# Expert gates: one-hot matmuls replaced by indirect DMAs that add chosen gates into zeroed DRAM tables

## The reference

```python
def peer_ffn(h, wq, subkeys, u, v):        # h: (1, 512, 1024)
    q = (h @ wq).reshape(B, T, 8, 2, 128)
    s = jnp.einsum('bthpd,pnd->bthpn', q, subkeys)      # 8 heads, 2 sides, 128 sub-keys
    s_top, i_top = lax.top_k(s, 16)
    cand = s_top[..., 0, :, None] + s_top[..., 1, None, :]        # 256 candidates
    cand_idx = i_top[..., 0, :, None] * 128 + i_top[..., 1, None, :]
    best, pos = lax.top_k(cand.reshape(B, T, 8, 256), 16)
    experts = jnp.take_along_axis(cand_idx.reshape(B, T, 8, 256), pos, axis=-1)
    gates = jax.nn.softmax(best, axis=-1)
    # y[t] = sum over the 128 picks k of  gates[t,k] * gelu(h[t] . u[e_k]) * v[e_k]
```

## Time and profile before

| | |
|---|---|
| times of three runs | 3919.15, 3919.49, 3920.51 us |
| span of the profiled execution, first to last instruction | 3916.3 us |
| PE busy | 3864.7 us, 99% of the span |
| DVE busy | 2781.5 us, 71% |
| ACT busy | 1523.5 us, 39% |
| POOL busy | 1321.6 us, 34% |
| mean granted TensorE clock | 0.997 |

### The profile page before, as it was taken

One profiled execution on the slowest core, in us unless ns is written; L12 is line 12 of the kernel. 1 busy time (PEld: TensorE's weight loads), 2 busy tenths in 40 slices (PEclk: granted clock), 3 DMA queues, 4 the chain that ended last, 5 costly groups with the idle time before them and its releaser, 6 DMA issues.

```text
span 3916.3 us, 48823 instructions
## 1 busy us (share of the span) xinstructions
PE 3864.7 (99%) x18074; PEld 3129.0 (80%) x18074; DVE 2781.5 (71%) x4585; ACT 1523.5 (39%) x2251; POOL 1321.6 (34%) x758
## 2 busy tenths in 40 slices
PE   7999999999999999999999999999999999999999
PEld 5767878888888888888877678788888888888887
DVE  5736557987777758888776363589787776588886
ACT  4537433343333333333344373433433333433332
POOL 2432333440000017777334223334300000387772
PEclk9999999999999999999999999999999999999999
DMA  7635333667776579999746432237677765899995
GB/s 286 226 124 170 113 128 108 226 228 263 266 260 222 204 260 391 364 359 358 269 162 222 134 130 81 82 118 242 232 260 262 258 241 180 305 376 372 353 354 198
DMA packets 411869, 918.97 MB, mean 235 GB/s; under 512 B 38416, under 2 KB 176528, under 8 KB 410032
## 3 DMA queue, kind: packets, MB, share of 16 engines
q1 hardware_dynamic: 327664, 664.77, 49.2%
q0 software_dynamic: 45056, 134.38, 9.2%
q10 hardware_dynamic: 38976, 117.66, 7.8%
HBM read 794.00 MB, written 256.90 MB: 268 GB/s over the span
## 4 chain that ended last, share of the span: by engine, by line
PE 83%; issue 7%; DVE 4%; POOL 4%; ACT 1%; DMA 1%; ACTq 0%; POOLq 0%; SPq 0%; DVEq 0%
PE ps L1057 14%; PE ps L1058 14%; PE ps L1059 14%; PE ps L1075 10%; PE ps L1077 10%; PE ps L1076 10%; POOL w_lo L1007 4%; PE ps L1432 2%; PE ps L1333 1%; PE ps L1337 1%; PE ps L1335 1%; PE ps L1300 1%; PE ps L1314 1%; PE ps L1290 1%; PE ps L1251 1%
## 5 line engine op out<-in xcount | busy, mean ns | idle before, releaser
L598 ACT ACTIVATE w_hi<-raw 128x1024 fp32r<-128x1024 f32 x504 | 534.3, 1060 | 1595.1 <-PE ps L1059 1316.1
L1057 PE MATMUL ps<-h_hi,w_hi 128*128 128x512 f32 x2768 | 1086.5, 393 | 5.1 <-POOL w_lo L1007 3.5
L1058 PE MATMUL ps<-h_hi,w_lo 128*128 128x512 f32 x2768 | 1080.1, 390 | 0.0
L1059 PE MATMUL ps<-h_lo,w_hi 128*128 128x512 f32 x2768 | 1079.5, 390 | 0.0
L1007 POOL TENSOR_TENSOR w_lo<-raw,w_hi 128x1024 fp32r<-128x1024 f32 x242 | 614.4, 2539 | 1101.1 <-ACT w_hi L598 1101.1
L1012 POOL DMA_INDIRECT acts<-expert_act,e_act x256 | 381.6, 1491 | 1244.9 <-DMA expert_act<-gel 1167.5
L1057 PEld LDWEIGHTS ps<-h_hi,w_hi 128*128 128x128 f32 x2768 | 519.2, 188 | 122.4 <-issue 8.9
L1059 PEld LDWEIGHTS ps<-h_lo,w_hi 128*128 128x128 f32 x2768 | 518.5, 187 | 112.2
L1058 PEld LDWEIGHTS ps<-h_hi,w_lo 128*128 128x128 f32 x2768 | 518.8, 187 | 100.9
L1867 DVE TENSOR_TENSOR w_lo<-raw,w_hi 128x1024 fp32r<-128x1024 f32 x192 | 235.1, 1224 | 277.1 <-ACT w_hi L598 277.1
L1020 POOL DMA_INDIRECT down<-expert_down,e_row x256 | 325.3, 1271 | 210.6 <-DVE y L2004 87.8
(11 more groups left out here) (288 smaller groups left out, 6070.2 us busy)
## 6 DMA issues: line engine op xcount, KB each, us to landing
raw<-in_stream_dram SPq DMA_DIRECT2D x648, 512.0 KB, 3.5
expert_down<-in_stream_dram SPq DMA_DIRECT2D x256, 512.0 KB, 5.2
expert_act<-gel ACTq DMA_DIRECT2D x256, 256.0 KB, 2.1
raw_more<-in_stream_dram SPq DMA_DIRECT2D x128, 512.0 KB
expert_gate<-gatebuf ACTq DMA_DIRECT2D x12, 4096.0 KB, 12.9
a_in<-expert_act SPq DMA_DIRECT2D x128, 384.0 KB
g_in<-expert_gate SPq DMA_DIRECT2D x128, 384.0 KB
ada_first<-in_stream_dram SPq DMA_DIRECT2D x8, 1024.0 KB, 17.9
```

The source lines that it names most:

```text
L598: return act.activation(o, i, ACT.Copy)
L1057: pe.matmul(o, w_hi[:, s, w], mov_hi[:, c, :], start=c == 0, stop=False)
L1058: pe.matmul(o, w_lo[:, s, w], mov_hi[:, c, :], start=False, stop=False)
L1059: mm = pe.matmul(o, w_hi[:, s, w], mov_lo[:, c, :], start=False, stop=c == KC - 1)
```

## The change

The one-hot matmuls, the transposes, the buffers and stores of the gate table are gone. In their place:

- SP clears a DRAM table for each layer, `expert_gate0` and `expert_gate1` (25 MB each), in 12 DMAs of 2 MB per layer, put between the unit loads from U_V to U_MIXB. The source is 256 KB of zeros in DRAM, read again and again in rows of 2 KB.
- DVE chooses the picks for two heads of all four tiles at once (`choose(g)`, g from 0 to 3), right after `experts_of` of these heads, and turns the exponentials into gates in `weigh(g)`, one pair of heads later. ACT takes the exponentials after the GELUs of units 16, 24, 32 and 41.
- POOL issues, from unit 16 of the U stage on, 384 indirect DMAs per layer (`add_gate`): each adds 128 gates, one for each token of a tile, to the table at the places that the picks name. Where a head follows another on the same tile, it waits until the earlier adds of that tile have landed. POOL now makes the lower halves of units 0 to 43, those of 16 to 43 in turn with the first adds; DVE makes them from 44 on.
- Before `load_pair`, SP waits for all adds to have landed.
- `g_in` is loaded in runs of 1536 B instead of 512 B.

```diff
+EXP_AT = (16, 24, 32, 41)
+SCATTER0 = 16
+LOW0 = 44
+CLEARS = 12
@@ sync @@
+            def clear_gates(l, n):
+                rows = gate_d[l].rearrange("(n p r f) o -> n p r (f o)", n=CLEARS, p=P, f=512)
+                sp.dma_start(rows[n], zero_d.unsqueeze(1).to_broadcast([P, NK * P * DSEQ // (CLEARS * P * 512), 512])
+                             ).then_inc(gate_cleared, 16)
...
                 load_split(l, U_U + 124, 0)
-                for half in range(2):
-                    sp.wait_ge(gate_stored[half], 16 + (l + 1) * DT * 16)
+                for tt in range(DT):
+                    sp.wait_ge(gate_added[tt], (l + 1) * PICKS * 16)
@@ scalar @@
+                        if e0 + b in EXP_AT:
+                            g = EXP_AT.index(e0 + b)
+                            act.wait_ge(gexp_in, l * 4 + g + 1)
+                            picks = best[:, :, 2 * g:2 * g + 2, :]
                             act.activation(picks, picks, ACT.Exp).then_inc(gexp, 1)
@@ gpsimd @@
+            def add_gate(l, n):
+                g, tt, k = n // (DT * 32), n // 32 % DT, n % 32
+                if tt == 0 and k == 0:
+                    pool.wait_ge(picked_ready, l * 4 + g + 1)
+                if k % TOPK == 0 and g * 2 + k // TOPK:
+                    pool.wait_ge(gate_added[tt], 16 * (l * PICKS + g * 32 + k))
+                h, c = 2 * g + k // TOPK, k % TOPK
+                pool.indirect_dma_start(out=gate_d[l],
+                                        out_offset=bass.IndirectOffsetOnAxis(ap=gate_i[:, tt, h, c:c + 1], axis=0),
+                                        in_=gate_v[:, tt, h, c:c + 1], in_offset=None, compute_op=ALU.add
+                                        ).then_inc(gate_added[tt], 16)
...
-                with pool.Fori(0, HOT0 // RAW) as i:
+                with pool.Fori(0, SCATTER0 // RAW) as i:
                     for b in range(RAW):
                         split(i * RAW + (l * N_SPLIT + U_U + b), b)
-                pool.wait_ge(index_ready, l + 1)
+                pool.wait_ge(gate_cleared, (l + 1) * CLEARS * 16)
+                lowered = SCATTER0
+                for n in range(DT * PICKS):
+                    if n % 3 != 2 and lowered < LOW0:
+                        split(l * N_SPLIT + U_U + lowered, lowered % RAW)
+                        lowered += 1
+                    add_gate(l, n)
@@ tensor @@
-                                for q in range(4):
-                                    o = ps[:, 4 + n % 2 * 2 + q // 2, q % 2 * 256:q % 2 * 256 + 256]
-                                    mm = pe.matmul(o, hot_j[:, n % HOT, q, :],
-                                                   hot_i[:, n % HOT, q].rearrange("p a b -> p (a b)"),
-                                                   start=True, stop=True)
@@ vector @@
+                for g in range(4):
+                    experts_of(2 * g)
+                    if g:
+                        weigh(g - 1)
+                    experts_of(2 * g + 1)
+                    choose(g)
+                weigh(3)
```

More of the change, by code:

```diff
@@ L163, in row_unit_of, with clears_by @@
     return ROW0 + k * (NK - 1 - ROW0) // PICKS
-def groups_before(e):
-    return e * 32 * DT // HOT_UNITS
+def clears_by(l, p):
+    first, last = PLACE[l]["w", U_V] - START[l], PLACE[l]["w", U_MIXB] - START[l]
+    return CLEARS * min(max(p - first + 1, 0), last - first) // (last - first)
 def pairs_lowered_at(n):
@@ L320, in trunk @@
     a_in = at("a_in", Z + 60, [P, 4, 2, DSEQ])
-    g_in = at("g_in", Z + 72, [P, 4, DSEQ // GT, 2, GT])
+    g_in = at("g_in", Z + 72, [P, 4, 2, DSEQ])
     y0 = at("y0", Z + 84, [P, D])
@@ L475, in load_listed @@
                         copy_down(l, n)
+                    for n in range(clears_by(l, p - 1) if p else 0, clears_by(l, p)):
+                        if l == 0 and n == 0:
+                            sp.wait_ge(zeros_stored, 16)
+                        clear_gates(l, n)
             sp.dma_start(silu_first[:], c_in).then_inc(c_loaded, 16)
@@ L973, in _ @@
-                for e0 in range(0, HOT_UNITS + 4, 4):
-                    experts(0, 4, HOT0 + e0, gates_after(e0))
+                with act.Fori(0, SCATTER0 // 4) as i:
+                    experts(i, 4, 0)
+                for e0 in range(SCATTER0, LOW0, 4):
+                    experts(0, 4, e0, gate_exp(e0))
+                with act.Fori(LOW0 // 4, 31) as i:
+                    experts(i, 4, 0)
                 def pair_hi(j):
@@ L979, in pair_hi @@
                     copy(g_hi[:, j // 4 % 2, j % 4 * 2:j % 4 * 2 + 2, :], a_in[:, j % 4]).then_inc(w_hi_ready, 1)
-                for e0 in range(HOT0 + HOT_UNITS + 4, 124, 4):
-                    experts(0, 4, e0, gate_exp(0) if e0 == 120 else None)
                 experts(0, 4, 124, pair_hi)
@@ L1846, in experts_of @@
                           lambda j: posi[:, j, h, :], TT)
-                for h in range(PH):
-                    experts_of(h)
-                def pick_rows(tt):
-                    dve.wait_ge(ghi_ready, l * DT + tt)
-                    dve.tensor_copy(idxT[:, tt, 2, :], g_round[:, tt, :].bitcast(F32))
-                    tt_op(idxT[:, tt, 3, :], ps[:, 4, 256:384], g_round[:, tt, :].bitcast(F32), ALU.subtract
-                          ).then_inc(idx_ready, 1)
-                lowered = HOT0
+                iota16 = const[:, C_IOTA:C_IOTA + TOPK].unsqueeze(1).to_broadcast([P, PICKS, TOPK])
@@ L1947, in add_lower @@
-                def add_lower(n):
-                    half, t = n // 16 % 2, 4 * (n % 16)
-                    dve.wait_ge(gate_upper, l * DT * 32 + n + 1)
-                    both = ps[:, 4 + n % 2 * 2:6 + n % 2 * 2, :].rearrange("p a (b i) -> p (a b) i", b=4)
-                    g4 = gatebuf[:, half, :, t:t + 4]
-                    tt_op(g4, both[:, 1:8:2, :].rearrange("p t i -> p i t"), g4, ALU.add).then_inc(gate_ready, 1)
-                one_hot(0)
-                for n in range(DT * 32):
-                    while lowered < HOT0 + HOT_UNITS and groups_before(lowered - 2 - HOT0) + 3 <= n:
-                        lower_next()
-                    if n < DT * 32 - 1:
-                        if n:
-                            dve.wait_ge(hot_ready, l * DT * 32 + n)
-                        one_hot(n + 1)
-                    weigh(n)
-                    if n >= 3:
-                        add_lower(n - 3)
@@ L1966, in _ @@
-                add_lower(DT * 32 - 3)
-                while lowered < HOT0 + HOT_UNITS + 2:
-                    lower_next()
-                add_lower(DT * 32 - 2)
-                add_lower(DT * 32 - 1)
-                dve.wait_ge(hot_ready, (l + 1) * DT * 32)
-                def lower_to_sum():
-                    while lowered < 124:
-                        lower_next()
-                pick_tile(0, lower_next, lower_to_sum)
+                for tt in range(DT):
+                    ins = dve.tensor_scalar(shift[:, tt, :], const[:, C_TOKEN:C_TOKEN + 1].to_broadcast([P, 32]), float(tt * P),
+                                            None, ALU.add)
@@ L1978, in product @@
+                step(ins)
+                for g in range(4):
[5 more added lines that the diff above has]
+                weigh(3)
+                while lowered < 124:
+                    lower_next()
                 def product(j):
@@ L1980, in product @@
                     dve.wait_ge(ag_loaded[b], 32 * (l * 16 + j // 4 + 1))
-                    a6 = a_in[:, b].rearrange("p i (c t) -> p c i t", t=GT)
-                    tt_op(a6, a6, g_in[:, b], ALU.mult).then_inc(w_prod, 1)
+                    tt_op(a_in[:, b], a_in[:, b], g_in[:, b], ALU.mult).then_inc(w_prod, 1)
                 def pair_lo(j):
```

227 lines of the change are left out of this document (64 added, 163 removed).

## The result

The changed kernel takes 4380.61 us (median of four runs, 4375.65 to 4386.92), the kernel before beside it 3919.32 (3918.54 to 3920.51). The ratio is 1.1177, 95% interval 1.1161 to 1.1193. The forecast of 4042 had the sign and the place right and less than a third of the size: 123 us of loss were forecast, 461 measured.

What follows compares the result with a forecast made beforehand. PE, busy 99%, was taken to bound the kernel. Per layer -51.7 + 9 + 4 + 90 + 5 + 5 = +61.3; two layers, +122.6 on the 3916.3 span, gave 4038.9, plus 3.2 for the median 4042 us; range 3880 to 4440.

Steps and rivals of the forecast that it cites:

- 51.7 us of one-hot matmuls: U stage of each layer: PE time for the gate table that the change removes, -51.7 us a layer.
- end stall: PE before unit 125, end of the U stage: waits for the gates and the loads behind them, 90 us a layer.
- The chain behind the adds: End of U stage: SP waits for all adds until 1461, then loads pairs and units 125 to 127; PE resumes at 1475.
- the low clock: After PE's stops: a lower granted clock for a moment, two stops a layer, 5 us a layer.
- The wait at unit 17: U stage: PE waits for unit 17's lower half, behind POOL's first add, 9 us a layer.
- the waits for landings: POOL after unit 43: eleven waits for an add just issued, 3.0 us each, 33 us; bounds 23 and 110.
- The other 344 adds: POOL's adds behind unit 43's lower half: 1.42 us each, 488 us for all.
- Rival 3: POOL's adds cost more than gathers: at 1.99 us each 197 a layer more, 4436 us, or 4696; chance 0.20.
- The price of disturbance: POOL's adds beside DVE's subtractions: 0.22 x 0.75 = 0.17 us more an add.
- rival 2: POOL's adds: DVE's subtractions don't slow them, 58 us a layer less, 3925 us; chance 0.12.
- The clears: Table clears in the queue that feeds PE: 12 transfers of 2 MB cost 5 us a layer; bounds 0 and 35.
- Units 17 to 43: U stage, where POOL mixes lower halves and adds: 4 us a layer of PE waits, bounds 0 and 24.

Runs made afterwards that it cites:

- two-tile run: Changed kernel with only tiles 1 and 2 added, 256 adds a layer instead of 384, tile 3's gates left out; 3889.92 us.
- the finer clears: Changed kernel with 48 clears of 512 KB from U_SQ to U_WQ instead of 12 of 2 MB from U_V to U_MIXB; 4353.02 us.
- the plain writes: Changed kernel with its 768 gate adds written plainly, without accumulation; 4691.97 us, and 4703.86 when run again.
- tiny memsets: Changed kernel with plain writes instead of adds and a 128x1 memset with a wait behind each on POOL; 4032.33 us.

## Why the prediction was wrong

**Right.** The kernel before was bound by PE, and 51.7 us of one-hot matmuls went from each U stage: in the two-tile run, where no end stall is left, the U stage of layer 0 took 704.5 us against 740.7, 36.2 less, with new waits of some 17 (in both layers 26.5 for POOL's halves and 6.9 for DVE's). The chain behind the adds is as told: 344 adds behind the lower half of unit 43, SP stopped, the pairs, units 125 to 127, and the low clock. The wait at unit 17 was given as 9 us and measured as 8.80, and the waits for landings as 33 us and measured as 30.7 (11 of them in layer 0). In the second there is luck: seven waits beside the weight stream took 3.4 us on the mean, and four during the end stall, when hardly anything else moved, 1.75.

**The step that failed** is the price in "The other 344 adds". I took the quiet gather, 0.95 + 0.30, and 0.17 for DVE; measured are 1.55 + 0.30 and 0.03. That is 0.45 more an add, 344 x 0.45 = 155 us in each layer. The gates were to be there at 1461 and SP went on at 1629: 17 us because the lower half of unit 43 ended at 954 instead of 937 (the U stage began 16.2 late), the rest is the price. The end stall came to 243 and 249 instead of 90. Rival 3 had the dearer add and priced it at 1.99 or 2.37; the measured 1.87 lies just below the first. Its reason, that an add "must name its destination for reading and for writing", isn't tested: the plain writes show that accumulating costs 0.59, not why. I took my value from the row that was nearest in kind, but that row did no accumulation, and I had put 0.20 on the rival and 0.42 on the value without one. That the measured time lies inside the stated range is due to this rival and not to the forecast's own sum.

**The price of disturbance.** By the Trainium skill, SBUF — State Buffer, section Who interferes with whom, a `tensor_tensor` of VectorE would not slow the writing of descriptors. This trace agrees on the mean, 0.03 us an add beside a subtraction in each 5.45 us, but not for single adds: twelve that began while a subtraction ran grew to between 1.79 and 2.60. My step from the gathers, 0.75 us times DVE's busy share, was wrong for this place, since most subtractions begin when an add is already under way and then cost it nothing. So rival 2 was nearly right on the disturbance and wrong on the time, because it too went by 1.25.

**The clears** were 16.2 and 18.0 us in a layer instead of 5, inside the bound of 35; the finer clears show that nearly all of it is theirs. I had counted on the loads' reserve to hide most of what a clear holds up, and it hid less. Of the 16.2 in layer 0, PE's waits for POOL's lower halves at line 1058 make 8.9.

**Units 17 to 43 and the clock** are, together with unit 17, what is left of the 206.5 of layer 0: 206.5 + 51.7 - 242.8 = 15.4, where I had 9 + 4 + 5 = 18. The trace splits it. PE's waits for POOL's lower halves in this U stage are 10.6 us in six, so 1.8 beyond the 8.8 of unit 17, where I had 4; the other 4.8 are left for the low clock and what no row names, where I had 5.

With the measured terms the sum for layer 0 is -51.7 + 15.4 + 242.8 + 16.2 = 222.7 instead of 61.3. Of the 161.4 between them 152.8 are the end stall and 11.2 the clears.

## What to carry to other kernels

An indirect DMA is not one price: before moving hundreds of them onto an engine's list, time one of the very kind (direction, accumulation) by itself, and multiply its duration and gap by the length of the queue behind the last thing that paces it. Ask for the last of the queue, not for the engine's busy share: POOL was at 34% and still too full, because the window in which the adds could run was shorter than they were; a part that fits the window (two tiles of three) wins where the whole loses. And a cheaper instruction isn't always safe: with plain writes at 1.26 us instead of adds at 1.85, TensorE, ACT and DVE were nearly stopped.

## What the runs showed of the hardware

- An accumulating indirect DMA of 128 elements holds POOL 1.55 us, a plain one 0.96 and a gather 0.94; the gap to the next is 0.30 in all three.
- Plain indirect writes of 128 single elements that follow each other at 1.26 us hold up TensorE, ACT and DVE: TensorE gets one instruction in 1.40 us, at 8% of DMA share. At 1.29 it is little better (281 matmuls in 420 us instead of 182; unhindered they are 1855), and at 1.35, with a memset of 0.11 us behind each, nothing of it is seen and the kernel took 4032 instead of 4704 us. That the mean rate over a few writes decides is shown by memsets behind every fourth one, long (nothing starved) and short (starved); the cause in the chip stays open. Gathers of this kind, run once, do the same (213 matmuls); adds, at 1.85, never come that close.
- A POOL add that began while a VectorE subtraction of two SBUF tiles was running took up to 2.60 us instead of 1.55; one that was already under way kept its 1.55.
- POOL waited 2.8 us on the mean for an add that it had just issued, 3.4 beside the weight stream and 1.75 without it. For a plain write it waited 1.4 where everything was starved and 2.7 where nothing was (tiny memsets), which fits the traffic beside them rather than the accumulation.
